# Two activation buffers (yh, yl) trade places in SBUF with the weight buffers, the residual, the constants and the parameters

## What is computed

```python
def first_block(x, ...):
    h = rmsnorm(x, norm1_g)
    (hg_q, hg_f, hg_i, hg_g, ml_qk, ml_v, ml_if, ml_o,
     mb_z, mb_xbc, mb_dt, gate_pre) = jnp.split(h @ w_in, split_at, axis=-1)
    ...                       # three recurrent branches: hgrn2, mLSTM, SSD -> y_hg, y_ml, y_mb
    mixed = (gates[0] * (y_hg @ w_br_hg) + gates[1] * (y_ml @ w_br_ml) + gates[2] * (y_mb @ w_br_mb))
    x = x + mixed @ w_out
    u = causal_dwconv(rmsnorm(x, norm2_g) @ w_up, ffn_conv_w, ffn_conv_b)
    x = x + (jax.nn.silu(u_g) * u_v) @ w_down
    return rmsnorm(x, final_g)

def second_block(x, ...):
    proj = rmsnorm_2(x, norm_w) @ w_in     # gated convolution inputs, q, k, v and gates
    ...                                    # dilated window attention, short gated convolution -> y
    return x + y @ w_out
```

## Time and profile before

| | |
|---|---|
| three runs | 1569.13, 1569.32 and 1569.76 us; median 1569.32 us |
| the profiled execution | 1568.92 us, of which 1567.1 us from the first to the last instruction |
| TensorE matmul busy | 1551.6 us, 99% |
| TensorE weight load busy | 1255.2 us, 80% |
| VectorE busy | 803.1 us, 51% |
| ScalarE busy | 725.4 us, 46% |
| GpSimd busy | 648.5 us, 41% |
| HBM read | 137.8 MB, 89 GB/s over the span |

### The profile page before, as it was taken

The page is one execution under the profiler, slowest core; times in us unless marked ns, Lnnn a source line. Parts: engine busy times, 40 slices in busy tenths (PEclk is TensorE's granted clock), DMA queues, the critical chain, the costliest instruction groups (busy, mean ns, idle before and its releaser), DMA issues.

```text
span 1567.1 us, 21409 instructions
## 1 busy us (share of the span) xinstructions
PE 1551.6 (99%) x7420; PEld 1255.2 (80%) x7420; DVE 803.1 (51%) x1383; ACT 725.4 (46%) x1160; POOL 648.5 (41%) x497
## 2 busy tenths in 40 slices
PE   7999999999999999999999999999999999999999
PEld 5888888888888888877777888888888887777777
DVE  4667767333455731577533344444442245656661
ACT  6666764323444432466644344444443234445551
POOL 5333333443333354333334444444455444343332
PEclk9999999999999999999999999999999999999999
DMA  6222222232222232222222322223233334222222
GB/s 239 81 68 81 67 70 79 88 96 86 74 74 68 80 94 94 81 68 81 67 78 87 95 93 96 92 96 94 96 94 102 107 123 160 67 81 68 68 68 94
DMA packets 39224, 140.89 MB, mean 90 GB/s; under 512 B 4264, under 2 KB 4520, under 8 KB 39152
## 3 DMA queue, kind: packets, MB, share of 16 engines
q1 hardware_dynamic: 37664, 135.02, 27.2%
q10 hardware_dynamic: 1488, 4.88, 0.8%
HBM read 137.76 MB, written 2.13 MB: 89 GB/s over the span
## 4 chain that ended last, share of the span: by engine, by line
PE 95%; DVE 3%; ACT 1%; issue 1%; DMA 0%; SPq 0%; DVEq 0%; ACTq 0%
PE bank L461 27%; PE bank L464 27%; PE bank L465 27%; PE bank L932 3%; PE bank L562 1%; PE bank L696 1%; PE bank L864 1%; PE bank L844 1%; PE bank L853 1%; DVE s_p L1949 1%; PE bank L665 0%; PE bank L615 0%; DVE s_e L1939 0%; DMA xs<-x 0%; PE bank L617 0%
## 5 line engine op out<-in xcount | busy, mean ns | idle before, releaser
L421 POOL TENSOR_TENSOR wl<-raw,wh 128x512 fp32r<-128x512 f32 x490 | 644.5, 1337 | 900.5 <-ACT wh L975 888.5
L461 PE MATMUL bank<-hh,wh 128*128 128x512 f32 x904 | 363.3, 402 | 0.1
L464 PE MATMUL bank<-hl,wh 128*128 128x512 f32 x904 | 356.7, 395 | 0.2 <-DVE hl L1531 0.2
L465 PE MATMUL bank<-hh,wl 128*128 128x512 f32 x904 | 356.6, 394 | 0.0
L461 PE MATMUL bank<-yh,wh 128*128 128x512 f32 x800 | 318.7, 398 | 0.7 <-DVE yl L1986 0.4
L465 PE MATMUL bank<-yh,wl 128*128 128x512 f32 x800 | 315.7, 395 | 0.0
L464 PE MATMUL bank<-yl,wh 128*128 128x512 f32 x800 | 315.6, 395 | 0.0
L975 ACT ACTIVATE wh<-raw 128x1024 fp32r<-128x1024 f32 x241 | 252.7, 1052 | 115.5 <-DMA raw<-slabs 114.7
L461 PEld LDWEIGHTS bank<-hh,wh 128*128 128x128 f32 x904 | 170.4, 188 | 39.8 <-issue 1.5
L465 PEld LDWEIGHTS bank<-hh,wl 128*128 128x128 f32 x904 | 170.1, 188 | 39.8
L464 PEld LDWEIGHTS bank<-hl,wh 128*128 128x128 f32 x904 | 170.4, 189 | 37.5 <-DVE hl L1531 0.5
(11 more groups left out here) (342 smaller groups left out, 1888.8 us busy)
## 6 DMA issues: line engine op xcount, KB each, us to landing
raw<-slabs SPq DMA_DIRECT2D x245, 512.0 KB, 3.5
wb<-bias_scratch ACTq DMA_DIRECT2D x1, 3584.0 KB, 13.8
xs<-x SPq DMA_DIRECT2D x4, 512.0 KB, 5.9
xT<-xt SPq DMA_DIRECT2D x4, 512.0 KB, 13.4
out<-a_l SPq DMA_DIRECT2D x4, 256.0 KB, 4.7
out<-au SPq DMA_DIRECT2D x4, 256.0 KB, 2.0
con<-consts ACTq DMA_DIRECT2D x1, 767.0 KB, 7.3
oneh<-onehot SPq DMA_DIRECT2D x1, 256.0 KB, 9.7
```

What stands on the lines that cost most here:

```text
L421: pool.tensor_tensor(slab(wl, i, half), slab(raw, i, half), slab(wh, i, half).bitcast(F32), ALU.subtract).then_inc(S["slab_split"], 1)
L461: mm(bank[:, :], wh[:, s, b, :], xh, start=first and i == 0, stop=False)
L464: mm(bank[:, :], wh[:, s, b, :], xl, start=False, stop=False)
L465: ins = mm(bank[:, :], wl[:, s, b, :], xh, start=False, stop=last and i == len(order) - 1)
```

## The change

The allocation order of the low part of SBUF is different. `yh` and `yl` (16 KB a partition each) come first, then `raw` with `wl` over it, `wh`, `xT` and the small ones. The first start is rounded up to a multiple of 256 bytes instead of 64. Every buffer from `hh` upwards keeps its place. No instruction is added, removed or put in another order: the instruction sequences of all five engines, with their waits, are the same in both kernels.

Offsets in bytes within a partition, as the allocator gives them (the first free one is 16481):

| buffer | before | after |
|---|---|---|
| `raw`, `wl` (16 KB, shared) | 16512 | 49408 |
| `wh` (16 KB) | 32896 | 65792 |
| `xT` (16 KB) | 49280 | 82176 |
| `con`, `par`, `zero` and six more small ones | 65664 | 98560 |
| `yh` (16 KB), over it `oneh`, `wrow` | 78080 | 16640 |
| `yl` (16 KB) | 94464 | 33024 |
| `hh` and all above | 110848 | 110848 |

The moved buffers between `raw` and `zero` go up by 32896 bytes, which is 32 KB and 128 bytes. Before, their starts leave a remainder of 128 when divided by 256; after, none. `yh`, `yl`, `hh`, `hl`, `fh` and `fl` start at multiples of 256 in both.

```diff
-        sb, sb_pos = arena(start)
+        sb, sb_pos = arena(-(-start // 256) * 256)
+        y_at = sb_pos[0]
+        yh = sb("yh", [P, KT, T], F32R)
+        yl = sb("yl", [P, KT, T], F32R)
         raw_at = -(-sb_pos[0] // 64) * 64
         raw = sb("raw", [P, 4, KT, P])
         wl = arena(raw_at)[0]("wl", [P, 4, KT, P], F32R)
...
         lbm = sb("lbm", [P, 8])
         lbt = sb("lbt", [P, 3, 8])
         sb_pos[0] = -(-sb_pos[0] // 256) * 256
-        y_at = sb_pos[0]
-        yh = sb("yh", [P, KT, T], F32R)
-        yl = sb("yl", [P, KT, T], F32R)
         h_at = sb_pos[0]
```

## The result

| | before | after |
|---|---|---|
| median of the runs | 1569.5 us | 1541.3 us |
| ratio | | 0.982, 95% interval 0.980 to 0.983 |
| profiled execution, first to last instruction | 1567.1 us | 1539.5 us |
| TensorE matmul busy | 1551.6 us | 1522.1 us |
| TensorE without a matmul (span less busy) | 15.5 us | 17.4 us |

The forecast was no change, 1569.3 us, with a range down to 1563. One of the four executions of after ran at a granted clock of 0.66 and took 2191.6 us; the ratio compares the other three (1541.0 to 1541.3 us) with before.

A forecast was written before the change was run, and what follows sets the result against it. TensorE's pace from matmul to matmul was taken as the bound. All terms summed to 0 against the profiled 1568.92 us; the forecast was the median, 1569.3 us, with a range of 1563 to 1575 us.

The forecast's parts named there:

- What bounds the kernel: Whole kernel: TensorE's pace from one matmul to the next sets the end; matmuls busy 1551.6 of 1567.1 us.
- TensorE streaming y: 2400 matmuls: pace doesn't follow the stream's place among three pairs of places; cost 0, bounds 2.2 us either way.
- TensorE loading weights: All 5640 slab matmuls: loads take 187 to 192 ns wherever weights lie, onr keeps the pace; cost 0.
- halves with the columns: onr's 256-column matmuls step at 0.12 us, half of 512 columns, so no visible fixed price per colliding weight load.
- list of signs: Profile after: unchanged paces, loads, writes and waits expected; shifted paces or a new TensorE wait for wl would show error.
- All three paces shifted together: Sign that the forecast is wrong: the slab matmuls' paces all change, read as the weights' place mattering.
- The two levels: Slab matmuls at 233.3 or 232.4 ns, read as phasing of loads and streams; all slow +4.2 us, all fast -0.8 us.
- Writes into y, the slab pipeline, xT and constants: ScalarE and VectorE writes, slab DMA, copy and split, small buffers: same durations or hidden behind TensorE; cost 0.
- Faster: a collision that the new distances lift: Slab matmuls: stream and weights collide, 19.1 ns a step; 108 us at most, 46 if only y profits; chance 0.14.
- Slower: the neighbours yl and wl: L465's loads read wl while L464 streams adjacent yl: 8 us, 1577 us; chance 0.14 together with the slow level.

The follow-up runs named there:

- a2_move_only: Order of after, y at 16640, but raw, wl, wh, xT and con 128 bytes further up, leaving 128 modulo 256; 1570.0 us, ratio 1.000 against before.
- a1_align_only: Order of before, only the first start rounded up to 256: raw, wl, wh, xT and con 128 bytes up; 1541.1 us, ratio 0.981 against before.
- a3_both_off: Order of before, weights still at 128 modulo 256, y, h and everything above moved down by 128 bytes; 1541.1 us, ratio 0.981 against before.

## Why the prediction was wrong

- *What bounds the kernel* was right. TensorE's pace sets the end, and 5.7 ns in a step of 232.4 moved the whole kernel by 1.8%. The pace from starts and counts was the reading that explained the result.
- *TensorE streaming y*, priced at 0: the price was right. `a2_move_only` gives it as 0 within 0.1%. The argument behind it was too narrow. Three places for the stream, one pace: but yh, fh and hh all stand at 0 modulo 256 and the slab weights at 128. I called them three different distances, and in the one respect that counts they were one.
- *TensorE loading weights*, priced at 0, is the step that failed. The runs show 5.7 ns a step in its place, for all three streams. In `a1_align_only` y stays where it was and the weights move by 128 bytes, with xT and the constants behind them: 29 us, the whole gain. I wrote that wh and wl had never been seen at a multiple of 256 and then let onr decide, which "stands 192 off". But hgph and hgpl, the streams of its matmuls, stand 192 off as well (223168 and 220096, onr at 228288): their difference is 0, the fast case, and I had compared a start where a difference counts. The two steps of 512 columns couldn't show it either. The rows have a resolution of 10 ns, and they are the first two after a change of weights, where slab steps aren't fast yet: in the trace they average 233 and 233 ns over eight such places in before, 229 and 233 in after. The duration of the loads, 188 ns in both kernels, says nothing about it; what changes is how far apart the matmuls start. The "halves with the columns" argument doesn't exclude a collision whose price grows with the time that a stream runs.
- The list of signs had the right one. "All three paces shifted together" is what the profile shows; its gloss, "the weights' place matters", is half of it, since in `a3_both_off` a shift of the streams alone has the same effect.
- *The two levels* were read as phasing, and that was a pointer. A pace that has several values with the same instructions and clock isn't a floor. After has 226.7 ns in all three stages, the one around 840 us included, where before had 233.3.
- *Writes into y, the slab pipeline, xT and constants* at 0: right, by the rows of after above.
- *The rivals.* "Faster: a collision that the new distances lift" was nearest to what the runs show, with 14% and a price of 46 to 108 us. Its span, 1566 down to 1461 us, takes 1541.3 in, but no price stands behind that place in it: 5.7 of the 19.1 ns came back, 29.5 us of matmul time. That it is a collision isn't shown. It ought to have had a middle case, and its evidence against should have weighed less, since it came from placements that weren't varied. "Slower: the neighbours yl and wl" is excluded by `a2_move_only`, where they are neighbours and nothing is lost.
- By the Trainium skill, "SBUF — State Buffer", section "Who interferes with whom", TensorE's stream and its weight loads have independent read ports. No run here shows the ports. The runs do show that the two don't go independently of their addresses: 226.7 to 234.3 ns with nothing else changed. The 216 ns of the Trainium skill, "TensorE: Matmul & The Clock Gate", section "Back-to-back issue gap", which that section gives for a matmul by itself, aren't reached by any placement tried. The best is 226.7 ns, and where the other 11 ns go stays open.

What isn't settled is the mechanism. That stream and load compete for a part of memory selected by the low 8 bits of the address would fit the period and the role of both kinds of weights, but no run separates it from other explanations, and it doesn't tell why 192 is good and 224 bad. Whether the effect goes when no weights are loaded beside a stream wasn't tried.

## What to carry to other kernels

Where TensorE is the bound, take the step from start to start over a few hundred equal matmuls and compare it between kernels; 5 ns are hard to read from durations of 395 ns that overlap, and invisible in single rows of 10 ns. For fp32r matmuls like these, let the starts of the weights and of every streamed operand leave the same remainder modulo 256 bytes: it costs some padding and was worth 1.8% here. Only 128x128 weights and streams of 512 columns were timed. Before calling a quantity independent of addresses, write down the remainders of the placements seen, of both operands; places far apart can be the same place.

## What the runs showed of the hardware

- The step of a 128x128 by 128x512 fp32r matmul in a long stretch depends on the difference between the weights' and the stream's start modulo 256 bytes: 226.7 ns at 0, 228.9 at 192, 232.4 to 233.3 at 128, 233.3 at 32, 64, 160 and 224, 234.3 at 96, all at a granted clock of 1.00 (2.4 GHz).
- With the difference kept, the remainders themselves made no difference (0 and 0, 128 and 128: 1541.3 and 1541.1 us), nor did a move by 32 KB (1570.0 against 1570.0 us).
- The first four slab steps after a small matmul are no faster at a difference of 0 than at 128 (307, 233, 232, 232 against 309, 232, 232, 231 ns); the fast pace is there from about the eleventh on.
- The weight load's own duration stays at 187 to 188 ns (median of each run); the busy times of the other engines stay within 1% over all runs (VectorE 801 to 807 us, ScalarE 725 to 726, GpSimd 648 to 653).
